# Where the split activations lie in a partition: chunks of 1024 bytes instead of 1088, at two fixed places modulo 256

## The reference, cut to what matters

```
y = gla_mixer(x, ...) if i == 0 else moba_mixer(x, ...)
x = layer_norm_2(DEEPNORM_ALPHA * x + y, ln_g[i, 0], ln_b[i, 0])
x = layer_norm_2(DEEPNORM_ALPHA * x + swiglu_ffn(x, w_gu[i], w_down[i]), ln_g[i, 1], ln_b[i, 1])

def swiglu_ffn(x, w_gu, w_down):
    gate, up = jnp.split(x @ w_gu, 2, axis=-1)      # 1024 -> 2 x 2816
    return (jax.nn.silu(gate) * up) @ w_down         # 2816 -> 1024
```

## Time and profile before

| | |
|---|---|
| median of 3 runs | 864.12 us (863.64 to 864.3) |
| the profiled execution | 864.27 us, span 862.5 us |
| TensorE busy | 850.2 us (99% of the span), 5390 matmuls |
| VectorE, ScalarE, GpSimd busy | 629.8, 426.5, 79.3 us |
| DMA | 154.46 MB, mean 179 GB/s |
| granted TensorE clock | 0.996 of full speed |

### The profile page before, as it was taken

How to read it: one execution, slowest core, us unless ns; L and a number is a source line. 1 busy time by engine, 2 the same in 40 slices (tenths; PEclk the granted TensorE clock), 3 DMA queues, 4 the chain that set the end, 5 groups by cost and what they waited for, 6 DMA issues and landing times.

```text
span 862.5 us, 13049 instructions
## 1 busy us (share of the span) xinstructions
PE 850.2 (99%) x5390; PEld 757.6 (88%) x5390; DVE 629.8 (73%) x880; ACT 426.5 (49%) x613; POOL 79.3 (9%) x81
## 2 busy tenths in 40 slices
PE   8999999999999999999999999999999999999996
PEld 7998999999988987878888988889988888889885
DVE  5999857688586675796777764678987777777445
ACT  6646454456664874435444453256553544445320
POOL 0340100122003001011000000031100200000000
PEclk9999999999999999999999999999999999999998
DMA  9963776664356752557556555386544765665531
GB/s 289 270 188 92 203 203 174 181 184 123 100 169 192 238 171 86 171 169 245 184 184 193 195 186 192 117 278 195 178 142 129 244 189 183 191 195 184 187 118 50
DMA packets 121989, 154.46 MB, mean 179 GB/s; under 512 B 11663, under 2 KB 98090, under 8 KB 121930
## 3 DMA queue, kind: packets, MB, share of 16 engines
q1 hardware_dynamic: 119978, 148.23, 56.4%
q0 software_dynamic: 1872, 5.26, 1.8%
q10 hardware_dynamic: 80, 0.13, 0.0%
HBM read 151.48 MB, written 1.05 MB: 177 GB/s over the span
## 4 chain that ended last, share of the span: by engine, by line
PE 94%; DVE 4%; DMA 1%; issue 0%; ACT 0%; SPq 0%; DVEq 0%
PE acc L597 19%; PE acc L599 19%; PE acc L598 19%; PE acc L635 15%; PE acc L639 8%; PE acc L720 1%; PE acc L717 1%; PE acc L718 1%; PE acc L668 1%; PE misc L798 1%; DMA x<-in_x 1%; DVE x L2191 1%; PE misc L857 1%; DVE y L2172 1%; DMA staged<-in_moba_w_in 1%
## 5 line engine op out<-in xcount | busy, mean ns | idle before, releaser
L1709 DVE TENSOR_TENSOR w_lo<-staged,w_hi 128x1024 fp32r<-128x1024 f32 (+1 forms) x274 | 331.6, 1232 | 134.6 <-ACT w_hi L1272 134.0
L1272 ACT CAST w_hi<-staged 128x1024 fp32r<-128x1024 f32 (+1 forms) x274 | 278.0, 1044 | 90.5 <-DMA staged<-in_ffn_w_down 44.2
L597 PE MATMUL acc<-x_parts,w_hi 128*128 128x256 f32 (+2 forms) x712 | 203.4, 286 | 0.0
L598 PE MATMUL acc<-x_parts,w_hi 128*128 128x256 f32 (+2 forms) x712 | 200.6, 282 | 0.0
L599 PE MATMUL acc<-x_parts,w_lo 128*128 128x256 f32 (+2 forms) x712 | 200.5, 282 | 0.0
L635 PE MATMUL acc<-x_parts,w_hi 128*128 128x512 f32 x576 | 196.3, 393 | 0.0
L639 PE MATMUL acc<-x_parts,w_lo 128*128 128x256 f32 x576 | 149.1, 279 | 0.0
L597 PEld LDWEIGHTS acc<-x_parts,w_hi 128*128 128x128 f32 x712 | 134.4, 189 | 1.7 <-issue 1.0
L598 PEld LDWEIGHTS acc<-x_parts,w_hi 128*128 128x128 f32 x712 | 134.0, 188 | 0.7 <-issue 0.2
L599 PEld LDWEIGHTS acc<-x_parts,w_lo 128*128 128x128 f32 x712 | 134.5, 189 | 0.0
L635 PEld LDWEIGHTS acc<-x_parts,w_hi 128*128 128x128 f32 x576 | 103.3, 188 | 18.4 <-DVE gate_sum L2352 0.2
(11 more groups left out here) (394 smaller groups left out, 1256.0 us busy)
## 6 DMA issues: line engine op xcount, KB each, us to landing
staged<-in_ffn_w_gu SPq DMA_DIRECT2D x88, 512.0 KB, 3.6
staged<-in_w_in SPq DMA_DIRECT2D x58, 512.0 KB, 3.8
staged<-in_ffn_w_down SPq DMA_DIRECT2D x44, 512.0 KB, 3.3
staged<-in_gla_w_in SPq DMA_DIRECT2D x24, 512.0 KB, 4.3
staged<-in_moba_w_in SPq DMA_DIRECT2D x24, 512.0 KB, 3.9
staged<-in_w_o SPq DMA_DIRECT2D x8, 512.0 KB, 3.9
staged<-in_gla_w_out SPq DMA_DIRECT2D x8, 512.0 KB, 3.8
staged<-in_moba_w_out SPq DMA_DIRECT2D x8, 512.0 KB, 3.8
```

Source lines behind the costliest of these rows:

```text
L597: pe.matmul(dst, st_hi, mv_hi, start=start, stop=False)
L598: pe.matmul(dst, st_hi, mv_lo, start=False, stop=False)
L1272: nc.scalar.copy(hi, raw).then_inc(rounded, 1)
L1709: nc.vector.tensor_tensor(lo, raw, hi, ALU.subtract).then_inc(split, 1)
```

## The change

The tile `x_parts` stays for the branches, now at an address that is a multiple of 256. Two more tiles are laid over the same bytes, one at that address (for x2 and x4, the FFNs' rows) and one 128 bytes further (for x1 and x3, the mixes' rows). In both a chunk is 256 positions, 1024 bytes, and chunks follow each other without a gap; the low half begins 8 x 272 x 4 = 8704 bytes after the high one. All readers and writers behind the branches use `high(tag)` and `low(tag)` or `ffn_split`. The ring's address is asserted to be 128 modulo 256, which it was before. Tiles under 256 bytes are now rounded to 32 bytes rather than 64. No instruction, wait or DMA is added or taken away.

```diff
-        cursor = [(nc.sbuf_base + 63) // 64 * 64]
+        cursor = [nc.sbuf_base]
+        def align(to):
+            cursor[0] = (cursor[0] + to - 1) // to * to
         def place(name, cols, dt=F32):
+            size = int(np.prod(cols)) * 4
+            align(64 if size >= 256 else 32)
             t = nc.alloc_sbuf_tensor_at(name, [P] + cols, dt, offset=cursor[0])
-            cursor[0] += (int(np.prod(cols)) * 4 + 63) // 64 * 64
+            cursor[0] += size
+        align(128)
         ring_at = cursor[0]
+        assert ring_at % 256 == 128
...
+        align(256)
+        parts_at = cursor[0]
         x_parts = place("x_parts", [2, KC, KEYS], F32R)
+        def split_at(past):
+            cursor[0] = parts_at + past
+            t = place("x_split%d" % past, [2, KC * KEYS], F32R)
+            return t[:, :, 0:KC * ROWS].rearrange("p s (k r) -> p k s r", k=KC)
+        ffn_split, mix_split = split_at(0), split_at(128)
+        cursor[0] = parts_at + 128 + 2 * KC * KEYS * 4
+        def split_of(tag):
+            return ffn_split if tag in ("x2", "x4") else mix_split
+        def high(tag):
+            return split_of(tag)[:, :, 0, :]
+        def low(tag):
+            return split_of(tag)[:, :, 1, :]
+        align(64)
...
+        align(128)
         region = cursor[0]
...
-  x_parts[:, :, k, 0:ROWS], start=k == 0, stop=k == KC - 1)
+  ffn_split[:, k], start=k == 0, stop=k == KC - 1)
...
-            xt_hi, xt_lo = x_hi[:, :, 0:ROWS], x_lo[:, :, 0:ROWS]
+            xt_hi, xt_lo = high("x1"), low("x1")
...
-                t_stage(..., xt_hi, xt_lo)
+                rows = "x2" if layer == 0 else "x4"
+                t_stage(..., high(rows), low(rows))
...
-                nc.scalar.copy(x_hi[:, lo:lo + n, t * P:t * P + P], ...
+                nc.scalar.copy(high(tag)[:, lo:lo + n, t * P:t * P + P], ...
```

More of the change, by code:

```diff
@@ L634, in with_both @@
                         def with_both():
-                            return pe.matmul(acc[:, p, b, :].rearrange("p (s n) -> p s n", s=2), hi[:, c, cols],
-                                             x_parts[:, :, k, 0:ROWS], start=k == 0, stop=k == KC - 1)
+                            return pe.matmul(acc[:, p, b, :].rearrange("p (s n) -> p s n", s=2), hi[:, c, cols], ffn_split[:, k],
+                                             start=k == 0, stop=k == KC - 1)
                         def with_high():
-                            return pe.matmul(acc[:, p, b, 0:ROWS], lo[:, c, cols], x_hi[:, k, 0:ROWS], start=False, stop=False)
+                            return pe.matmul(acc[:, p, b, 0:ROWS], lo[:, c, cols], ffn_split[:, k, 0, :], start=False, stop=False)
                         if k == 0:
@@ L716, in n_first @@
                                     if part == 0:
-                                        pe.matmul(dst, xt_hi[:, k, rows], w_hi[:, sl.ring(), cols], start=k == 0, stop=False)
-                                        pe.matmul(dst, xt_hi[:, k, rows], w_lo[:, sl.ring(), cols], start=False, stop=False)
+                                        pe.matmul(dst, high(tag)[:, k, rows], w_hi[:, sl.ring(), cols], start=k == 0, stop=False)
+                                        pe.matmul(dst, high(tag)[:, k, rows], w_lo[:, sl.ring(), cols], start=False, stop=False)
                                     else:
-                                        mm = pe.matmul(dst, xt_lo[:, k, rows], w_hi[:, sl.ring(), cols], start=False,
+                                        mm = pe.matmul(dst, low(tag)[:, k, rows], w_hi[:, sl.ring(), cols], start=False,
                                                        stop=k == KC - 1)
@@ L1128, in swiglu @@
                 wide_stage(FIRST[tag] + 6, COUNT[tag] - 10, OUT["up%d_1" % layer])
-                t_stage(FIRST[tag] + COUNT[tag] - 4, 4, OUT["gate%d_%d" % (layer, LAST_H)], xt_hi, xt_lo)
+                rows = "x2" if layer == 0 else "x4"
+                t_stage(FIRST[tag] + COUNT[tag] - 4, 4, OUT["gate%d_%d" % (layer, LAST_H)], high(rows), low(rows))
                 tag = "down%d" % layer
@@ L1477, in round_rows @@
                 await_full(act, name)
-                nc.scalar.copy(x_hi[:, lo:lo + n, t * P:t * P + P], bank(name)[:, 0:n * P]
+                nc.scalar.copy(high(tag)[:, lo:lo + n, t * P:t * P + P], bank(name)[:, 0:n * P]
                                .rearrange("p (c r) -> p c r", c=n)).then_inc(s["x_rounded"], 1)
@@ L2115, in rest_rows @@
                 dve.wait_ge(s["x_rounded"], 5 * (int(tag[1]) - 1) + u + 1)
-                read(rest(x_lo[:, lo:lo + n, t * P:t * P + P], bank(name)[:, 0:n * P].rearrange("p (c r) -> p c r", c=n),
-                          x_hi[:, lo:lo + n, t * P:t * P + P]), name)
+                read(rest(low(tag)[:, lo:lo + n, t * P:t * P + P], bank(name)[:, 0:n * P].rearrange("p (c r) -> p c r", c=n),
+                          high(tag)[:, lo:lo + n, t * P:t * P + P]), name)
             dve.wait_ge(s["gain_scaled"], 1)
@@ L2515, in rest_tile0 @@
                     await_read(pool, "%s_%d" % (tag, j))
-                    nc.gpsimd.tensor_tensor(x_lo[:, 4 * j:4 * j + 4, 0:P], y[:, 0, j * 512:j * 512 + 512]
-                                            .rearrange("p (c r) -> p c r", c=4), x_hi[:, 4 * j:4 * j + 4, 0:P].bitcast(F32),
+                    nc.gpsimd.tensor_tensor(low(tag)[:, 4 * j:4 * j + 4, 0:P], y[:, 0, j * 512:j * 512 + 512]
+                                            .rearrange("p (c r) -> p c r", c=4), high(tag)[:, 4 * j:4 * j + 4, 0:P].bitcast(F32),
                                             ALU.subtract).then_inc(s["x_rest"], 1)
```

## The result

The changed kernel takes 866.08 us in the median (865.52 to 866.53), the kernel before beside it 863.67 (863.42 to 864.32). The ratio is 1.0025 with a 95% interval of 1.0016 to 1.0034: slower by a quarter of a percent, where 860.6 was forecast. That is rival 2 in sign, and in size within 0.6 us of its 866.6.

What follows compares the result with a forecast made beforehand. TensorE, busy 850.2 of 862.5 us, was taken as the bound, through matmul start distances. Terms -2.7, -0.7, -0.3, +0.2, -0.2, +0.1 sum to -3.6 us: 864.27 to 860.7, stated as 860.6; range 858.4 to 864.3.

Steps and rivals of the forecast that it cites:

- rival 2: A fixed place repeats one bad meeting of reads: FFN wide pairs +2.3 us, mixes' 256-column matmuls +1.0, total 866.6; chance 0.09.
- (a): FFN wide stage, 576 matmul pairs, x always at place 0: 343.7 ns per pair instead of 348.35, -2.7 us.
- Rival 1: Start distances only shift between neighbours, their sum ignoring place: FFN wide and 256-column stages unchanged, 863.4 us; chance 0.20.
- (e): 256-column `t_stage`s: mixes held at place 128, -0.2 us (bounds -0.4 to +1.0); FFNs' last four slots +0.1.
- (b): Mixes' `n_slots`, 192 matmuls of 512 columns, x stationary at place 128: 227.4 ns instead of 230.9, -0.7 us.
- (c): Mixes' `n_first`, 96 matmuls of 512 columns with x stationary: from about 231 ns to 227.6, -0.3 us.
- (d): FFNs' `n_first`, 96 matmuls with x stationary at place 0: some 233 ns against 231.2, +0.2 us.
- (f): Branches, `x_parts` moved from place 192 to 0, each slot still meeting all four places: 0, give or take 0.3 us.
- (g): Writers of the split rows, and small tiles lying 192 bytes on: taken as nothing, 0.2 us either way estimated.
- Rivals 1 and 3: The first: place leaves the sum unchanged, 863.4 us, chance 0.20; the other: pair locks near 339 ns, 857.9, chance 0.05.

Runs made afterwards that it cites:

- places_a: Changed kernel with the split rows at other standing places: x1 at 0, x2 and x3 at 64, x4 at 128; 865.57 us, ratio 1.0021 to the kernel before.
- places_b: Changed kernel with x1 and x2 standing at place 192, x3 at 128, x4 turning as before; 865.55 us, ratio 1.0021 to the kernel before.
- ring_192: Changed kernel, every tile and the ring 64 bytes on; relative to it x1, x2 as changed, x3 as in places_a, x4 as before; 863.93 us, ratio 0.9999.
- mixes_64: Changed kernel with x1, x3 standing at place 64, x2, x4 in 1088-byte chunks, low half 64 bytes further; 859.74 us, ratio 0.995 to the kernel before.

## Why the prediction was wrong

The failed step is (a), and in it one choice: "I take 343.7, what place 0 costs while the others lie around it". With the place standing the pair takes 351.2 in place of 343.7 (350.8 with the stalled pairs left out, as they are in 343.7). The stages came out at +0.59 and +0.72 where the step had -2.7, and the stretch that was to take 93.6 us takes 95.5, with a round of three where all pairs were to be alike. Its bounds of 339 to 357 held the value; the point chosen in them did not. The distances of the earlier trace rows belong to the round as a whole and are not the prices of single places. The change, places_a and places_b together show this directly: all four standing places are dearer than the mean of the four turning ones. Rival 1, a sum that no place changes, fell with it.

(e) failed in the same way. The price of place 128 amid others (354 per three) gave -0.2; standing, three take 360.0, the upper bound that the step named. The mixes measured +0.39 and +0.57, the FFNs' last slots +0.14 twice instead of +0.1 in all.

(b) was right in kind and two thirds of its size: -0.34 and -0.09 instead of -0.7. The lock at 226.7 came, but some six matmuls at about 231 ahead of it weigh more in a run of slots that begins after other work. (c) and (d) were nearly nothing: -0.05 and -0.06 for the mixes, +0.02 twice for the FFNs, though the pace of the earlier trace rows did rise as (d) had it; what covers it in these stages was not tested. TensorE in the first FFN's `n_first`, the same 15 matmuls:

```profile
376.32 0.39 PE L747 MATMUL acc<-w_lo,x_split 128*128 128x512 f32 x1
...
379.81 0.40 PE L749 MATMUL acc<-w_hi,x_split 128*128 128x512 f32 x1
```

3.49 us, some 233 ns each (before 230.7). For (f), the way to the GLA is 0.10 us shorter, nearly all of it by 10.5 us, before the branches' first product; the products themselves take the same. (g) can't be told apart: the output and down stages, which had no other term, are 0.11 longer in all.

The terms sum to 1.31 - 0.43 - 0.11 + 0.04 + 0.96 + 0.28 - 0.10 + 0.11 = 2.06 us; the profiled executions differ by 866.34 - 864.27 = 2.07. So nothing is left over, and no wait was added.

Rival 2 had the sign and one of its two sizes: +1.0 for the 256-column lock at 120 (measured 0.96, at 120.0 to the nanosecond). For the pair it had +2.3 (measured 1.3), and the pair stayed just under the 351.5 ns from which it was to decide. That its total of 866.6 came so near is partly luck: what the pair fell short by was made up in part by (b) to (d), which gained less than it took, and by the last slots' +0.28. Its picture, one dear meeting repeated, holds for the 256-column stages and not for the pair, which keeps a round of three. It was held down to 0.09 by "place 0 is the cheapest of the four in rows 4", the same inference that broke (a): one assumption carried the forecast and the argument against its main rival. The earlier trace rows had stood for it, and for 256 columns alone it held: x1 at 0 in places_a runs at 118.5 to 119.0 ns, as there. But 118.75 is no cheaper than the turning stage's 118.3; it never showed that a cheap place stays cheap, nor anything of the pair. (Rivals 1 and 3 add up to 863.3 and 857.8, each 0.1 under what the prediction has; nothing hangs on it.)

Settled by the runs: the FFN's part alone makes the change slower, through the pace of TensorE, and that pace depends on how the operands' places lie to one another (ring_192). That places count modulo 256 is borne out in the kernel before: chunks k and k + 4 are alike modulo 256 but not modulo 512, and their pairs agree within 0.7 ns (344.0 and 343.3 at place 0). Open: the rule. Neither place by place, nor the bytes of distance, nor the gap between the halves foretells a standing rate, and the 256-column matmul can run at two with the same places.

## What to carry to other kernels

A distance from start to start in a mixed stream is a property of the sequence; before a layout is fixed on its cheapest member, run that member alone, since here the cheapest of four became dearer than their mean. Where TensorE is busy for 99% of the span, operand addresses modulo 256 relative to the weights are worth a handful of runs (from 0.25% slower to 0.5% faster here, with the same instructions), and they must be tried, stage by stage, rather than derived. A gain in the pace of the busiest engine can come back as waits for the next one, as VectorE shows here, so the layouts are compared by undisturbed slots before they are ranked by time. If one assumption holds up the forecast and strikes down its rival, their chances belong closer together.

## What was not expected of the hardware

A 256-column matmul of this type holds 120.0 ns at a distance of 0 between the places of the two operands, and 113.3 at -64 (places_a, mixes_64; in ring_192 11 of the 16 slots run at 117.8), for the same instruction at a granted clock of 1.00. In ring_192 GLA and the FFNs kept their paces with all places moved by 64. The Trainium skill, "TensorE: Matmul & The Clock Gate", section "Part 2: What happens when you issue a matmul", has the two operands read through independent ports. A difference of 6.7 ns by the operands' distance does not agree with reads that have no part in each other, though no run here shows where they meet.

A stream can hold either of two paces with the same places (117.8 and 113.4 ns in places_b), and a standing place can still run in a round of three (the change). Both would fit a pace that depends on what the matmuls before left behind; no run here tests it.
